# Ten more tokens of the third tile go to the fetched-row path of a hybrid decoder block, with a new order around the hand-over

## The reference

```
q = (hf @ w_query).reshape(T, PEER_HEADS, 2, PEER_HALF)
s = jnp.einsum('thpd,hpkd->thpk', q, sub_keys)
s1, i1 = lax.top_k(s[:, :, 0], 16);  s2, i2 = lax.top_k(s[:, :, 1], 16)
best, pos = lax.top_k(s1 + s2 over all 256 pairs, 16)      # idx = i1 * 128 + i2
gate = softmax(best)
...
u = expert_u[ib];  act = einsum('td,thkd->thk', hb, u)
wgt = gb * gelu(act);  vv = expert_v[ib]
out = einsum('thk,thkd->td', wgt, vv)
```

## Time and profile before

| what | value |
|---|---|
| median of 3 runs | 4116.03 us (4115.01 to 4121.3) |
| profiled execution, own time | 4116.04 us |
| its span | 4114.3 us |
| mean granted TensorE clock | 0.998 |
| busy: PE / VectorE / ScalarE / GpSimd | 99% / 53% / 34% / 59% |
| HBM read and written | 864.41 MB and 64.00 MB |

### The profile page before, as it was taken

How to read it: one execution, slowest core, us unless ns; L and a number is a source line. 1 busy time by engine, 2 the same in 40 slices (tenths; PEclk the granted TensorE clock), 3 DMA queues, 4 the chain that set the end, 5 groups by cost and what they waited for, 6 DMA issues and landing times.

```text
span 4114.3 us, 54344 instructions
## 1 busy us (share of the span) xinstructions
PE 4067.4 (99%) x21875; PEld 3688.9 (90%) x21875; DVE 2170.0 (53%) x2854; ACT 1401.8 (34%) x1756; POOL 2420.6 (59%) x768
## 2 busy tenths in 40 slices
PE   8999999999999999999999999999999999999998
PEld 7888888877877888888899999999999999999997
DVE  4300035121122011207888888888437888888885
ACT  4322222332333121223345555555332222232233
POOL 4444443433433434443357777777778888888883
PEclk9999999999999999999999999999999999999999
DMA  4233322222222433323248999999989999999993
GB/s 184 94 123 121 117 102 94 97 82 82 93 82 82 163 115 115 118 92 133 92 165 331 346 345 344 346 347 344 366 340 384 398 381 384 382 385 381 390 364 133
DMA packets 210813, 929.39 MB, mean 226 GB/s; under 512 B 18672, under 2 KB 96816, under 8 KB 111408
## 3 DMA queue, kind: packets, MB, share of 16 engines
q1 hardware_dynamic: 64080, 460.35, 30.4%
q0 software_dynamic: 46080, 335.56, 20.8%
q10 hardware_dynamic: 100576, 132.56, 9.0%
HBM read 864.41 MB, written 64.00 MB: 226 GB/s over the span
## 4 chain that ended last, share of the span: by engine, by line
PE 93%; POOL 2%; DVE 2%; ACT 1%; DMA 1%; issue 1%; ACTq 0%; SPq 0%; DVEq 0%; POOLq 0%
PE bank L1952 16%; PE bank L1953 15%; PE bank L1954 15%; PE bank L1992 8%; PE twin L1992 8%; PE bank L2296 4%; PE twin L2296 4%; PE twin L2298 4%; PE bank L2298 4%; PE twin L2297 4%; PE bank L2297 4%; POOL low L575 1%; PE twin L2267 1%; PE twin L1953 1%; PE twin L1954 1%
## 5 line engine op out<-in xcount | busy, mean ns | idle before, releaser
L575 POOL TENSOR_TENSOR low<-raw,high 128x2048 fp32r<-128x2048 f32 x351 | 1629.2, 4642 | 1447.4 <-ACT high L684 1263.4
L684 ACT ACTIVATE high<-raw 128x2048 fp32r<-128x2048 f32 x190 | 363.9, 1915 | 1220.6 <-PE bank L1954 737.7
L1952 PE MATMUL bank<-x_pack,high 128*128 128x352 f32 x1952 | 630.9, 323 | 8.6 <-POOL low L575 8.6
L1952 PE MATMUL bank<-x_high,high 128*128 128x512 f32 x1632 | 636.9, 390 | 0.0
L1954 PE MATMUL bank<-x_high,low 128*128 128x512 f32 x1632 | 635.0, 389 | 0.0
L1953 PE MATMUL bank<-x_low,high 128*128 128x512 f32 x1632 | 635.0, 389 | 0.0
L1953 PE MATMUL bank<-low_pack,high 128*128 128x352 f32 x1952 | 629.7, 323 | 0.0
L1954 PE MATMUL bank<-x_pack,low 128*128 128x352 f32 x1952 | 629.5, 323 | 0.0
L696 ACT ACTIVATE high<-raw 128x2048 fp32r<-128x2048 f32 x162 | 310.5, 1917 | 737.6 <-PE twin L2298 433.6
L1952 PEld LDWEIGHTS bank<-x_pack,high 128*128 128x128 f32 x1952 | 367.3, 188 | 10.7 <-issue 6.3
L1953 PEld LDWEIGHTS bank<-low_pack,high 128*128 128x128 f32 x1952 | 367.3, 188 | 0.0
(11 more groups left out here) (301 smaller groups left out, 7336.2 us busy)
## 6 DMA issues: line engine op xcount, KB each, us to landing
raw<-weights SPq DMA_DIRECT2D x353, 1024.0 KB
raw_values<-weights SPq DMA_DIRECT2D x42, 1024.0 KB
raw_experts<-weights SPq DMA_DIRECT2D x38, 1024.0 KB
act_dram<-act_out ACTq DMA_DIRECT2D x128, 176.0 KB
retrieved_dram<-stage ACTq DMA_DIRECT2D x44, 512.0 KB
act_in<-act_dram ACTq DMA_DIRECT2D x32, 704.0 KB
gates_in<-retrieved_dram ACTq DMA_DIRECT2D x32, 704.0 KB
gates_dram<-sgu_act ACTq DMA_DIRECT2D x32, 256.0 KB, 2.0
```

Source lines behind the costliest of these rows:

```text
L575: nc.gpsimd.tensor_tensor(low[:, slot, :], rounded, high[:, slot, :].bitcast(F32), ALU.subtract).then_inc(low_done, 1)
L684: nc.scalar.activation(high[:, slot, :], raw[:, slot, :], ACT.Copy).then_inc(high_done, 1)
L1952: nc.tensor.matmul(o, high[:, slot, w], xh, start=(k == 0), stop=False)
```

## The change

`EXTRA` goes from 32 to 42, so `COLS` is 342 and three groups of 42 use 126 of the 128 partitions, with 43 rows each for U and V. `LATE` falls from 16 to 6, `LEAD` grows from 12 to 18, so `FIRST_STEP` is 20; 86 gate steps do. VectorE looks up tile 3 first, tells GpSimd at once (`listed_done`), and does 16 early dots in five batches between the other lookups and the set-up. GpSimd fetches from the ninth expert unit on, into four places of which three are new; afterwards it uses six. One of the new places is `raw_experts`, so SP's first load there waits for `rows_used` 16. The tables are turned in two parts, with unit e18 between them, through other PSUM banks. The last rows of the value stage are spread to v120 instead of v117.

```diff
-ROW_BUFS = 4
+ROW_BUFS = 6
+FETCH_FROM = 8
-EXTRA = 32
+EXTRA = 42
-STAGES = COLS // STAGE_TOK
+STAGES = -(-COLS // STAGE_TOK)
-LEAD = 12
+LEAD = 18
+GATE_STEPS = -(-COLS // WTOK)
+LAST_STEPS = GATE_STEPS - STEPS * (STAGES - 1)
+EARLY = 16
+EARLY_DOTS = (2, 4, 7, 11, EARLY)
-LATE = 16
+LATE = 6
-EXTRA_GAP = 2
+EXTRA_GAP = 1
...
-    return min(U_ROWS, max(0, unit - FIRST_STEP) * U_ROWS // (ETILES - FIRST_STEP - 4))
+    return min(U_ROWS, EARLY + max(0, unit - FIRST_STEP) * (U_ROWS - EARLY) // (ETILES - FIRST_STEP - 4))
+def early_by(unit):
+    slow, fast = min(unit, 15) - FETCH_FROM + 2, 2 * max(0, unit - 15)
+    return min(EARLY, slow + fast)
...
-    return min(V_ROWS, early + max(0, unit - begin) * (V_ROWS - LATE) // (ETILES - 10 - begin))
+    return min(V_ROWS, early + max(0, unit - begin) * (V_ROWS - LATE) // (ETILES - 7 - begin))
...
+        if n < EARLY:
+            b = (0, 8, 9, 10)[n % 4]
+        elif n < U_ROWS:
+            b = (1, 2, 3, 0, 8, 9)[(n - EARLY) % ROW_BUFS]
+        else:
+            b = (n - U_ROWS) % VALUE_BUFS
...
                 elif place == 2 and before is None:
                     sp.wait_ge(unit_done, FIRST_UNIT + LEAD)
+                    sp.wait_ge(rows_used, LOANED)
...
-                if n >= ROW_BUFS:
-                    pool.wait_ge(rows_used, n - ROW_BUFS + 1)
+                b, _, before = ROW_PLACES[n]
+                if before is not None:
+                    pool.wait_ge(rows_used, before + 1)
...
-                if n == LEAD + 1:
+                if n == FETCH_FROM:
                     pool.wait_ge(listed_done, 1)
-                if n > LEAD:
-                    wanted = min(U_ROWS, dots_by(n) + ROW_BUFS - 1, fetched_u + (1 if n < LEAD + 4 else 2))
+                    pool.wait_ge(unit_done, FIRST_UNIT + PACKED + 1)
+                if n == FIRST_STEP + 1:
+                    pool.wait_ge(tables_done, 1)
+                if n >= FETCH_FROM:
+                    wanted = early_by(n) if n <= FIRST_STEP else min(U_ROWS, dots_by(n) + ROW_BUFS - 2, fetched_u + 2)
...
-            act.wait_ge(slots_turned, 1)
-            for src, dst in ((4, idx1_t), (5, idx2_t), (6, gate_high)):
-                ins = nc.scalar.activation(dst[:], bank[src][:, 0:DENSE], ACT.Copy)
-            ins.then_inc(slots_kept, 1)
+            for n, kept in enumerate((((2, idx1_t), (3, idx2_t)), ((2, gate_high),))):
+                act.wait_ge(slots_turned, n + 1)
+                for src, dst in kept:
+                    ins = nc.scalar.activation(dst[:], bank[src][:, 0:DENSE], ACT.Copy)
+                ins.then_inc(slots_kept, 1)
...
+            look_up(DENSE_T)
+            then(nc.vector.scalar_tensor_tensor(out=slot_i[:], in0=expert_i[:, 0, DENSE_T, :], scalar=float(KEYS),
+                                                in1=expert_i[:, 1, DENSE_T, :], op0=ALU.mult, op1=ALU.add))
+            dve.sem_inc(listed_done, 1)
+            dve.wait_ge(gffn_in, 16)
+            then(nc.vector.tensor_tensor(wide[:], xb[:, DENSE_T, :], gffn_all[:], ALU.mult))
+            for n, t in enumerate((2, 0, 1)):
+                look_up(t)
+                dots_until(EARLY_DOTS[n])
...
+            dots_until(EARLY_DOTS[3])
+            dve.wait_ge(slots_kept, 2)
+            then(nc.vector.tensor_tensor(gate_low[:], bank[2][:, 0:DENSE], gate_high[:].bitcast(F32), ALU.subtract))
+            dve.sem_inc(tables_done, 1)
...
             gate_hits(0)
             dve.wait_ge(extra_saved, 16 * 2)
+            dots_until(EARLY_DOTS[4])
...
+            turn_slots((2, expert_i[:, 0, :, :]), (3, expert_i[:, 1, :, :]))
+            column(0, cols=COLS)
+            pe.wait_ge(slots_kept, 1)
+            turn_slots((2, all_best[:].rearrange("p t h k -> p t (h k)")))
+            column(1, cols=COLS)
```

More of the change, by code:

```diff
@@ L1190, in stage_units @@
                 index = s * STEPS + FIRST_STEP
-                for q in range(STEPS):
+                n_steps, gap = (STEPS, 2) if after else (LAST_STEPS, 1)
+                for q in range(n_steps):
                     expert_unit(q % 2, index + q, high=ring_high)
-                    if before and q % 2 == 0:
-                        keep_stage(s - 1, 1 - half, q // 2)
-                    if after or q < STEPS - 1:
+                    if before and q % gap == 0 and q // gap < PIECES:
+                        keep_stage(s - 1, 1 - half, q // gap)
+                    if after or q < n_steps - 1:
                         gate_parts((q + 1) % 2, s * STAGE_TOK + (q + 1) * WTOK)
@@ L1698, in _, with take, dot, dots_until @@
             then(nc.vector.tensor_copy(pos_f[:], pos_half[:]))
-            for t in range(TT):
+            taken, dots = Count(), 0
+            def take():
+                n = taken.next() - 1
+                b, uses, _ = ROW_PLACES[n]
+                dve.wait_ge(rows_in[b], 16 * uses)
+                return fetched[b]
+            def dot(n):
+                extra, which = ROW_ORDER[n] if n < U_ROWS else (False, SLOTS - LATE + n - U_ROWS)
+                where = take()
+                by, sums = (wide_extra, extra_act) if extra else (wide, slot_act)
+                nc.vector.scalar_tensor_tensor(out=where[:], in0=where[:], scalar=1.0, in1=by[:], op0=ALU.mult,
+                                               op1=ALU.mult,
+                                               accum_out=sums[:, which:which + 1]).then_inc(rows_used, 1)
+            def dots_until(n):
+                nonlocal dots
+                while dots < n:
+                    dot(dots)
+                    dots += 1
+            def look_up(t):
                 for p in range(2):
@@ L2277, in _ @@
             gate_pair(first=True)
[L2278 removed]
+            with repeat(pe, GATE_STEPS // 2 - 1, *column_pair, (made, 2), (outs, 2)):
                 gate_pair()
```

122 lines of the change are left out of this document (56 added, 66 removed).

## The result

Six runs of the changed kernel have a median of 4132.91 us (4127.23 to 4135.63), six of the kernel before beside them 4118.03: ratio 1.003 (95%: 1.002 to 1.004), slower by 0.3%. The forecast was 4073 us. The profiled execution took 4135.63 us; its span is 19.6 us longer than that in the earlier trace rows.

The account below looks back on a forecast made before the run. PE was taken to bound the kernel; from the profiled 4116.04 us, terms from -50.8 for columns to +8.0 for the sparse sum's end totalled -43.2, giving 4073 us (range 4058 to 4095).

Parts of the forecast that it names:

- Columns, -50.8: Expert and value units: 12192 matmuls with ten columns less, 4.17 ns each on a straight line, save 50.8 us.
- 32-column rival: Rival, 5%: PE charges columns in steps of 32, so the column gain goes; some 4124 us.
- steps of eight: Matmul widths: if the array charged steps of eight columns (344), the column term would be -40.6 us.
- Six places, -9.8: Gate stretch: six row places end eight late `low` waits, 1.25 us each; 9.8 us saved, between 0 and that.
- Hand-over, +5.8: Tables' hand-over: row 15's fetch waits for dot 11 and delays `low` of e20; 5.8 us lost (4 to 11).
- turning and ACT's copy: T+1.0: Hand-over: the second table turning and ACT's copy are done 1.0 us after the end of e18, called T.
- The 80 us at 425 GB/s say that this fits: DMA traffic: gated units need 375 GB/s and value units 393, judged to fit because 425 was held.
- End of the sparse sum, +8.0: Value stage's end: ACT waits for the later sparse sum, PE loses 9.4 us in place of 1.4; +8.0 (5 to 10).
- GpSimd in the value stage, +5: Value stage: about 24 units with two fetches and `low` cost 0.2 us each; +5 (0 to 10).
- VectorE's banks, +1: Value stage: VectorE at 89% of its time may free banks late at a few group borders; +1 (0 to 5).
- Fewer late rows (-4.5): Head of the value stage: the double row rate ends after three or four units; 4.5 us saved (0 to 5).
- units ahead of the gates (+3.1): Six more units before the gates: ACT's table loads make `low` of even units late; 3.1 us lost.

Follow-up runs that it names:

- e18: Not a run: an expert unit of the kernel; the second turning of the tables is done by PE only after it.
- x1: Changed kernel with the 43 dots of the dense tokens' rows reading the sparse tile's vector in PSUM (wrong sums, same work): 4112.66 us, ratio 0.9986.
- e24: Not a run: the expert unit whose `low` begins the timed gate stretch, 673.2 us to that of e105 in the changed kernel.
- e105: Not a run: the expert unit whose `low` ends the timed gate stretch, 673.2 us from that of e24 in the changed kernel.
- x14: x9 with the dense tokens' dots reading the sparse tile's vector in PSUM (wrong sums, same work): 4081.34 us, ratio 0.9907.
- x15: x9 as a whole kernel with the 43 dense rows behind the 122 sparse ones, vectors exchanged between so the one in use is in PSUM: 4093.34 us.
- e20: Not a run: an expert unit at the hand-over; its `low` stands behind row 15's fetch in GpSimd's queue.
- x8: Changed kernel, last-stage stores every second unit, sparse sum up to three units earlier, early rows one a unit to the fourteenth, gate sum before dots: 4111.52 us.
- x2: Changed kernel with the last stage's four pieces stored behind every second unit of the trail, not each: 4125.64 us, ratio 1.002.
- x16: x15 with the last stage's pieces stored behind every third unit of the trail, not every second: 4078.68 us, ratio 0.9900.
- x4: Changed kernel with the sparse sum's rows spread up to three units earlier, as before the change: 4121.04 us, ratio 0.9997.
- x9: Changed kernel, stores every second unit, sparse sum up to three units earlier, early rows one a unit, moving tiles' starts moved: 4119.8 us, ratio 0.9998.
- two sweeps: Kernels of matmuls alone, no other engine at work, varying widths and tile starts: 342 columns from element 4 took 153.32 ns in one, 155.97 in another.

## Why the prediction was wrong

The profiled spans differ by +19.6 us where the sum said -43.2. Its terms, one by one:

- **Columns, -50.8: the step that failed.** "I take the line" between 512 and 352 columns. With tiles from element 0 the line holds at 512, 384, 320 and 256 columns (288 is 1.6 ns under it), but not at the places that the changed kernel has for its 342, where it says 155.8 and 157.8 and 158.9 were measured. Units fell by 0.11 to 0.12 us in the expert stage and by some 0.04 in the value stage: 122 x 0.12 + 128 x 0.04 is about -20. The 32-column rival is out as well; steps of eight gave -40.6 and would also have been too much. 31 us.
- **Long dots: not in the sum.** The step that failed is the silent one that a dot always takes 2.28 us and a `low` 4.64. The row of the dots is a mean over those with the vector in PSUM. Three of the five long units lose 3.7 to 4.0 us and two 2.4, two followers 0.7 each, and the eight units behind a stretched `low` 0.5 each: 22 us, the same as x1 took off between e24 and e105. x14 and x15 bear it out.
- **Six places, -9.8: right, a little large.** No 9.41 us unit is left. Before there were seven in the gate stretch, not eight (and eight times 1.25 would be 10.0); they cost 8.6 us. But the stalls that went were fewer microseconds than what took their place. 1 us.
- **Hand-over, +5.8: right in mechanism, too small.** The fetch of row 15 waited for dot 11 and held `low` of e20, as written. The step "turning and ACT's copy: T+1.0" failed: ScalarE stood 3.38 us for weights ahead of that copy. With 8.6 us at e20, 0.9 before a gate step soon after and 2.0 by the clock it is about 12. One row a unit and the other order took it down: from `low` of e0 to that of e24 it is 206.5 us in the changed kernel, 196.9 in x8.
- **Trail: not in the sum.** Eight pieces of stages in ten units met full DMA engines and held up ScalarE's queue. The step that failed is "The 80 us at 425 GB/s say that this fits": those 80 us moved whole rows and weights, and with the pieces the share is 1.03 at 381 GB/s. 9 us (x2, x16).
- **End of the sparse sum, +8.0: right, a little small.** A gap of 10.8 us in place of 1.2, and 1.3 by the clock: 10.9 (x4: 10.7 of span).
- **GpSimd in the value stage, +5, and VectorE's banks, +1:** neither came; the units shrank by 0.05 us there and not by 0.2. Fewer late rows (-4.5) and the units ahead of the gates (+3.1) came as written.

31 + 22 + 1 + 6 + 9 + 3 - 6 is 66 for the 62.8 us between forecast and span; e0's `low` started 2.0 us sooner than before (2045.4, 2047.4), and I leave the last microsecond open. Of the rivals none happened as a whole. The DMA engines bound in the trail and, by late weights, at the hand-over, but not in the value stage, where 391 GB/s and in x9 402 went with a PE that never stood.

Left open: what rule sets the pitch. That the starts of the tiles move it was shown in two sweeps and inside the kernel; but two equal cases in two sweeps differ by 2.65 ns, and the kernel before goes through 161.1, 158.9 and 160.0 ns in one stage with nothing moved.

## What to carry to other kernels

Before a line through two widths is used for a third, time that width with the tiles where the kernel has them: ten columns of 352 gave 2.2 ns or 1.1 where 4.2 were expected. Look at the place of both inputs of every VectorE instruction that works beside GpSimd: two in SBUF are a wait of up to GpSimd's whole instruction, and a mean duration taken while the phases happened to differ does not show it. A gap of 2.0 us before a gate step cost 2.4 us, and 3.7 where the clock halved behind it; and where several waits replace one, undo them one at a time, since each is small and only together do they turn the sign.

## What the hardware showed that I had not expected

- The pitch of fp32r matmuls of one width between 153.3 and 160.0 ns by the start of the moving tile, with no other engine at work; 338 columns at the price of 336, 346 above 348. And 352 columns at 161.1, 158.9 and 160.0 ns in one stage of one run.
- VectorE instructions of 0.68 and 2.28 us stretched to 5.07 and 6.34 behind GpSimd's subtraction, with both inputs in SBUF, and never with one in PSUM (165 dots in x16, 36 of which began while `low` ran); GpSimd's subtraction of 4.6 us stretched to 6.7 behind such a dot.
- Half the granted clock for up to some 5 us of matmuls behind gaps of 2.0 to 10.8 us, but not behind every gap of 2 us.
- A 0.46 us issue on ScalarE's DMA queue that took 12.45, a 171 KB store that landed 29.3 us after its issue, and DMA engines that are full at 381 GB/s with the stages' pieces among the traffic, having moved 425 without them.
